# Sample's key products of a head pair placed in chunks 17 to 19 in place of 18 to 20

## What is computed

```
z = rms_norm(x) @ w_in                      # 2048 x 6144: u, g_pool, q, k, v, g_attn
pool = (trailing mean of u over 2/4/8/16 positions - u) @ pool_w * scale
attn = softmax(q k / 8 - slope * distance, three dilated patterns) @ v   # 16 heads x 64
x = x + concat(pool * silu(g_pool), attn * silu(g_attn)) @ w_out         # 2048 x 2048
y = rms_norm(x)
```

## Time and profile before

| | us |
|---|---|
| median of 3 runs | 910.71 |
| the profiled execution | 908.99 |
| its span, first to last instruction | 907.2 |
| TensorE busy | 861.7 (95%) |
| VectorE busy | 566.5 (62%) |
| ScalarE busy | 402.5 (44%) |
| GpSimd busy | 52.4 (6%) |

### The profile page before, as it was taken

How to read it: one execution, slowest core, us unless ns; L and a number is a source line. 1 busy time by engine, 2 the same in 40 slices (tenths; PEclk the granted TensorE clock), 3 DMA queues, 4 the chain that set the end, 5 groups by cost and what they waited for, 6 DMA issues and landing times. The chain is left out here.

```text
span 907.2 us, 17338 instructions
## 1 busy us (share of the span) xinstructions
PE 861.7 (95%) x7014; PEld 848.5 (94%) x7014; DVE 566.5 (62%) x1035; ACT 402.5 (44%) x896; POOL 52.4 (6%) x96
## 2 busy tenths in 40 slices
PE   6899999999999999999999999999989999999991
PEld 6799999999999999999999999999979999999990
DVE  4555767677677767667786767686689633333322
ACT  5545434523553454355236434543546434344332
POOL 3000000001000100000010001000000000000000
PEclk9999999999999999999999999999999999999996
DMA  8354266354536543563555366335475334334324
GB/s 289 94 151 124 80 149 172 100 133 135 142 97 146 167 120 93 135 171 103 130 151 133 93 155 174 102 97 156 135 196 165 114 114 122 115 116 122 110 60 188
DMA packets 207048, 121.36 MB, mean 134 GB/s; under 512 B 7576, under 2 KB 201760, under 8 KB 206432
## 3 DMA queue, kind: packets, MB, share of 16 engines
q1 hardware_dynamic: 202520, 111.20, 44.4%
q0 software_dynamic: 4448, 9.05, 3.2%
HBM read 108.04 MB, written 12.63 MB: 133 GB/s over the span
## 5 line engine op out<-in xcount | busy, mean ns | idle before, releaser
L546 PE MATMUL pj<-mov_hi,w_hi 128*128 128x260 f32 x2048 | 423.6, 288 | 8.2 <-DVE w_lo L1101 7.8
L546 PE MATMUL pj<-mov_hi,w_lo 128*128 128x260 f32 x2048 | 412.9, 283 | 0.0
L546 PE MATMUL pj<-mov_lo,w_hi 128*128 128x260 f32 x2048 | 412.2, 283 | 0.0
L546 PEld LDWEIGHTS pj<-mov_hi,w_hi 128*128 128x128 f32 x2048 | 316.1, 189 | 10.7 <-DVE mov_lo L1122 4.4
L546 PEld LDWEIGHTS pj<-mov_lo,w_hi 128*128 128x128 f32 x2048 | 316.5, 189 | 0.0
L546 PEld LDWEIGHTS pj<-mov_hi,w_lo 128*128 128x128 f32 x2048 | 316.2, 189 | 0.0
L1101 DVE TENSOR_TENSOR w_lo<-w_raw,w_hi 128x640 fp32r<-128x640 f32 (+1 forms) x192 | 166.4, 867 | 214.1 <-ACT w_hi L744 213.2
L744 ACT ACTIVATE w_hi<-w_raw 128x640 fp32r<-128x640 f32 (+1 forms) x192 | 147.6, 769 | 184.2 <-PE pj L546 183.9
L804 ACT ACTIVATE pt_hi<-ps_t 128x128 fp32r<-128x128 f32 (+1 forms) x64 | 26.2, 435 | 77.4 <-PE ps_t L554 71.8
L1183 DVE TENSOR_TENSOR pt_lo<-ps_t,pt_hi 128x128 fp32r<-128x128 f32 (+1 forms) x64 | 29.7, 484 | 41.3 <-ACT pt_hi L804 41.3
L788 ACT ACTIVATE arena<-arena,stat 128x128 f32<-128x128 f32 (+1 forms) x64 | 35.5, 555 | 35.9 <-DVE stat L1169 35.8
(11 more groups left out here) (161 smaller groups left out, 709.5 us busy)
## 6 DMA issues: line engine op xcount, KB each, us to landing
w_raw<-in_w_in SPq DMA_DIRECT2D x96, 320.0 KB, 3.3
w_raw<-in_w_in SPq DMA_DIRECT2D x48, 384.0 KB, 3.6
arena<-in_cache_k_win SPq DMA_DIRECT2D x16, 384.0 KB, 5.2
arena<-in_cache_v_win SPq DMA_DIRECT2D x16, 384.0 KB, 8.2
w_raw<-in_w_out SPq DMA_DIRECT2D x16, 384.0 KB, 3.7
w_raw<-in_w_out SPq DMA_DIRECT2D x16, 320.0 KB, 3.0
arena<-row_scratch POOLq DMA_DIRECT2D x8, 512.0 KB, 5.2
arena<-in_cache_k_win SPq DMA_DIRECT2D x8, 512.0 KB, 6.4
```

What stands on the lines that cost most here:

```text
L546: mm = pe.matmul(pj[a][h][:, 0:HT], w, m[:, k, HT * h:HT * h + HT], start=(k == 0 and i == 0), stop=(c == 2 and k == KT - 1 and i == 2))
```

## The change

The plan of pairs 0 to 6 places the three key products one chunk earlier. Everything else in the plan stays, `sample_bias` in chunk 20 too. `FINAL`, the plan of pair 7, is not touched.

```
-USUAL = Plan(qk=(7, 12), s=(8, 13), kn=13, ur=15, kq=(18, 19, 20), ns=20, pt=22,
+USUAL = Plan(qk=(7, 12), s=(8, 13), kn=13, ur=15, kq=(17, 18, 19), ns=20, pt=22,
              vm=(23, 23, 24), va=(24, 25), av=26, mix=(19, 21), gate=20)
 FINAL = Plan(qk=(7, 11), s=(8, 12), kn=15, ur=17, kq=(12, 13, 14), ns=14, pt=16,
              vm=(18, 18, 19), va=(19, 19), av=20, mix=(17, 18), gate=19)
```

## The result

The changed kernel took 905.61 us, the median of six runs (905.34 to 907.25), beside 910.62 (909.37 to 913.6) for the kernel before. The ratio is 0.9944, with a 95% interval of 0.9927 to 0.9961. The forecast was 905.4. In a second series it had 905.76 us beside 912.29, ratio 0.9933 [0.9919, 0.9947].

The account below looks back on a forecast made before the run. TensorE was taken as the bound, busy 861.7 of 907.2 us. Seven pairs' turns gaining 0.76 us each give 5.3, so 910.71 less 5.3 is 905.4 us; range 903.7 to 909.5.

Parts of the forecast that it names:

- The chain: VectorE's step 20: output halves, third product and sum, then the bias TensorE's turn awaits; moving the product saves 2.50 us there.
- The rule that was weighed: At the turn of line 554: a gap repeating alike may mean too little SBUF or PSUM; then gain 0. Trace spoke against it.
- Its size: Turn of line 554: 0.76 us per pair by starts, 5.3 us over seven pairs; 4.2 by the idle column.
- The replay: VectorE's instructions from 431.69 us in the even pair, re-timed with old spacings: bias ends at 444.95 at the latest, 0.95 earlier.
- the margin: Even pair's turn: bias needed by 445.14 us, ready 0.19 to 0.30 us before that.
- The median: Whole kernel: 910.71 less 5.3 gives 905.4 us; the median was taken as 1.72 us above the profiled execution.
- The chances: Whole kernel against a measurable difference of about 0.5%: faster 0.51, same 0.43, slower 0.06.
- The even pairs' rival: Bias still late in pairs 0, 2, 4, 6: about 0.3 us wait each, 906.6 us, or 908.4; chance 0.16.
- The value loads: Behind chunk 22's split: last load issued at about 445.4 us, landed by 454.0, wanted at 456.62 less 0.76.
- Pair 7: Last pair, with the other plan: its 2.5 us wait of line 554 stays alone; the sum has no term for it.

Follow-up runs that it names:

- run 1: Against the kernel before, only the third key product moves, from chunk 20 to 19 behind the second; 907.36 us beside 910.39, ratio 0.9956.
- run 2: Against the kernel before, the first two key products move one chunk earlier, the third stays in chunk 20; 910.39 us beside 910.39, ratio 1.0002.
- run 4: Changed kernel with line 1194's instruction executed three times instead of once in chunk 20 of pairs 0 to 6; 911.39 us beside 910.74 for the kernel before.
- run 9: Changed kernel with the second fold of the sample's values in chunk 24 instead of 25, pairs 0 to 6; 901.73 us beside 912.29 for the kernel before.
- run 11: Against the kernel before, key products one chunk earlier in pairs 0 to 5 only, pair 6 left as before; 907.31 us beside 912.29, ratio 0.9943.
- run 6: Against the kernel before, key products one chunk earlier in pairs 4 to 6 only; 909.79 us beside 910.74, ratio 0.9987.
- run 7: Changed kernel with the last pair's first key product in chunk 11 instead of 12; 906.55 us beside 910.74 for the kernel before, ratio 0.9958.
- run 8: Changed kernel with the second value fold in chunk 24 (pairs 0 to 6) and the last pair's first key product in chunk 11; 902.51 us beside 910.74.
- run 3: Changed kernel with all three key products one chunk earlier still, in chunks 16 to 18; 907.16 us beside 910.39 for the kernel before, ratio 0.9948.
- run 5: Against the kernel before, key products one chunk earlier in pairs 0 to 2 only; 909.01 us beside 910.39, ratio 0.9977.

## Why the prediction was right, and where it was off

**The chain.** Right, by runs 1, 2 and 4 together: the third product in chunk 20 is what the turn waited for, the other two are worth 0.25 us in an even pair, and the slack behind the move is as sharp as a chain's. The rule that was weighed, of the Trainium skill (Perfetto Trace Analysis, Optimization Strategy), that a gap which repeats alike can be a want of buffers, does not describe this gap: it repeated seven times, and went with no buffer added.

**Its size.** 0.76 us a pair were forecast and 0.77 measured in the windows of pairs 2 and 3; up to pair 7's turn it is 5.12 us of the 5.3. The idle column alone (0.60) would have given 4.2 us; the starts gave the right number. The replay ended 0.23 us too late in pair 4, since a sum whose follower needs nothing of it lets it start 1.14 us after its own start (429.93 to 431.07 above), while I took 1.25. So the margin was larger than I said: the bias ends 0.56 us before the turn, of which 0.14 are the way to TensorE, so 0.42 in place of 0.19 to 0.30.

**The median** met the forecast to 0.2 us, and that is in part luck. The sum had no term for pair 7, where 1.5 us were lost in the profiled execution. What made up for it is the step from profile to median: I took the 1.72 us of the kernel before for both kernels. In the comparison it was 1.63 for that one and 0.21 for the changed one. (The chances add up to 0.44 for the same time and 0.05 for slower, where I wrote 0.43 and 0.06.)

**The even pairs' rival** came true in one pair. Pair 6 keeps 0.19 us: its bias ends 0.15 us before the turn, and the turn starts 0.43 us after the last matmuls.

```profile
605.27 0.40 PE L546 MATMUL pj<-mov_hi,w_lo 128*128 128x260 f32 x2
605.70 0.49 PE L554 MATMUL ps_m<-tab,arena 128*16 128x128 f32 x3
```

I had replayed pair 4 for all even pairs. In pair 6 VectorE begins chunk 19's split (line 1101) 1.49 us after its last piece of work, not 1.21, and some 0.6 us later beside TensorE. One sum more (line 1272) stands in step 16 there, and the reciprocal behind it comes later, for which ScalarE waits before it makes the w_hi:

```profile
589.87 0.72 ACT L796 ACTIVATE arena<-arena,stat 128x512 f32<-128x512 f32 x1 [0.49 <-DVE stat L1177]
```

**The value loads** were off. I had the last one going out near its old time and landing 1.9 us before its use. SyncE issued all three in a row behind chunk 22's split, and the slowest of pair 4 took 10.7 us in place of 8.6:

```profile
DMA to landing us min/median/max: 7.4/8.0/10.7
```

VectorE waited for it, before its first value product in pair 4 and, for 0.55 us, in pair 6:

```profile
453.86 2.36 DVE L1228 TENSOR_TENSOR arena<-arena 128x1024 f32<-128x1024 f32 x2 [0.94 <-DMA arena<-in_cache_v_win]
...
460.47 0.96 DVE L1101 TENSOR_TENSOR w_lo<-w_raw,w_hi 128x768 fp32r<-128x768 f32 x1 [0.58 <-ACT w_hi L744]
```

It cost nothing, because VectorE's idle time in chunk 25 took it up: 0.58 us are left of the 1.59 there before. Line 699's wait is 0.33 as ever.

**Pair 7** I took to be untouched. Its own instructions are, but 1.5 us were lost there in the profiled execution. Eleven profiles have pair 7's plan as it was. By the time of its turn:

| turn of pair 7 at | kernels | low clock lies | turn to end |
|---|---|---|---|
| 663.4 | folds only | behind the first wait | 236.7 |
| 665.4 to 669.8 | changed (twice), pairs 0 to 5, third only, one more, pairs 4 to 6 | behind the second | 238.1 to 238.2 |
| 670.2 to 672.5 | pairs 0 to 2, before, two only, two extra | behind the first | 236.7 to 236.8 |

Both explanations by the pairs ahead are refuted (runs 9 and 11). So what fits is *when* in the execution the two waits come. But the bands are drawn from these same eleven single executions, and run 6 moved an edge: the last two bands are 0.4 us apart there (669.77 and 670.18). No run shifted the time alone. What sets the place of the low clock stays open.

A second thing moves whole executions, and it lies in the start of the kernel, ahead of the first pair's turn. Pair 0's turn, less what it waited from start to start, comes at 115.7 to 116.0 us in six of the thirteen profiles (before, changed twice, runs 2, 7 and 8), and at 117.1 to 118.8 in the others. Three of these (runs 3, 5 and 9) have one more stretch at 1.2 GHz some 34 to 38 us after the start, and mean clocks of 0.983 and 0.984. The executions of the kernel before at 0.983 may have it too; no trace of one is kept. The two profiles compared above began alike to 0.1 us, and both lack it.

Of the kernel before, executions without the lower clock lie near 909.0 us (8 of 38), near 910.3 (25) and between 911.5 and 911.9 (5); its profile is of the first of these groups. The 1.3 us between the first two could be a later start, as in runs 1, 4, 6 and 11, or the loss in pair 7; no trace of such an execution is kept. That is how 3.6 us in the profiles and 4.8 to 6.5 in the medians can stand beside the 5.1 up to pair 7's turn.

## What to carry to other kernels

Find the instruction that the bounding engine waits for, and take out of the chain in front of it what needs not be there; move it in front of an idle time of its own engine. Work beside that chain brings little when it is moved: two of these three products brought 0.25 us in an even pair, and one chunk too early they cost 0.8 us in pair 6 (run 3). Replay the row of starts, for every kind of repetition and not for one, and price a wait from start to start, not by the idle column; here that decided between 4.2 and 5.3 us.

## What the runs showed of the hardware that I had not expected

- In pair 7 a stretch of some 3.4 us at 1.2 GHz, behind a TensorE wait of 1.8 or 3.4 us, cost nothing where a long wait for another engine followed it (2.53 in place of 3.40 us), and 1.5 us where none did.
- The length of a wait did not settle whether the clock fell. Waits of 0.60 us, and one of 1.51 us (run 4), left it at 1.00. The same wait of 2.39 us, some 32 to 35 us after the start of all thirteen profiles, was followed by the low clock in three of them (runs 3, 5 and 9) and not in the other ten.
- Of two long waits 9 us apart only one was followed by the low clock in each of eleven profiles; with the first one of 2.47 us, and 13 us ahead of the second (runs 7 and 8), both were.
- A wait of 0.25 us on TensorE does not show in the idle column at all, since it lies under the modelled ends; two starts show it (0.49 in place of 0.24 us, run 1).
